# Part of the block attention moved into the projection loop of a hybrid decoder layer

## The chip, the cores and the metric

The kernel runs on all 8 cores of one Trainium2 chip. Each core computes one batch element and no data pass between cores. The metric is the device time of the slowest core, in microseconds (us).

## The reference, cut to what matters

For one batch element, `x` is 2048 tokens by 1024 features. One input projection of 5120 columns feeds three head groups (mLSTM, MoBA block attention, attention to 256 memory tokens). Each group is multiplied by a SiLU gate, the results are concatenated, and one output projection and a layer norm follow. The change touches the MoBA group:

```
proj = x @ w_in
x_m, z_m, q_a, k_a, v_a, z_a, q_c, z_c = split_cols(proj)
qa, ka = rotary(q_a), rotary(k_a)                  # 4 heads of 128
# keys in 8 blocks of 256; each query sees its own block (causal) and the
# 3 past blocks with the largest q . mean(k of the block)
out_a = moba_attention(qa, ka, va) * silu(z_a)
```

A query in the first four blocks has at most three past blocks, so for tokens 0 to 1023 nothing has to be selected. Selection concerns tokens 1024 to 2047 only.

## The kernel before, in words

The kernel is written with a small scheduler (class `Sched`): each call of `S.add` appends an instruction to the list of one engine, in the order in which the Python code runs, and puts in the semaphore waits that reads and writes of named tiles ask for. So each engine runs its instructions in program order, and an instruction that waits holds up everything behind it on its engine. All matmuls go through `mm` (L233), all activations through `act` (L236), and most DMAs through `dma` (L239), so many rows carry the line of a helper.

The work of a core comes in five parts with barriers between them: (1) the projections for MoBA, then the MoBA attention itself (up to L555); (2) memory attention (to L638); (3) the rest of the mLSTM projections; (4) convolution and gates; (5) the mLSTM recurrence and the output. The change is in part 1 alone.

**Projections** (L387 to L400). `fm_tile` makes one tile of 128 features by 512 tokens with 8 matmuls into one of PSUM banks 0 to 3, in turn; `va_tile` makes a V tile of 128 tokens by 512 features in the same way. `j` counts four chunks of 512 tokens, `c` four groups of features (for `fm_tile` one head each). A Q tile (`wA`, `evq`) or K tile (`wC`, `evk`) is evacuated by `ev_rot`: three VectorE products with the cosine and sine tables (L367 to L369, PSUM and SBUF in), then one GpSimd addition (L370, both inputs in SBUF) that writes `qa` or `ka`. A V tile is copied by ScalarE (L385). A gate tile (`wD`, `evz`) is evacuated by ScalarE with SiLU. Chunk 0 is made first, then for `j` = 1 to 3 and `c` = 0 to 3 one tile each of Q, V, K and gate.

**Attention** (L431 to L553). `T` counts four chunks of 512 queries. For each `T` and head there are 2(2T+1) items 'w' (128 keys against the 512 queries) and one item 'n' (the last 256 keys against the upper 256 queries): 3, 7, 11 and 15 items a head, 144 in all, 40 of them with T below 2. An item is: scores (one matmul, plus causal masks, plus for T of 2 and 3 a matmul with `esel` that adds the selection mask `selT`), an exponential on ScalarE into `Ebuf`, a PV matmul into bank 6, and an addition into `Esum` on VectorE (L531 to L540). Scores run two items ahead, in banks 0 to 2. After each head comes the head end (L546 to L553): a matmul with ones sums `Esum` over partitions (bank 7), ScalarE takes Ln, copies bank 6 to `osb` and takes Exp, and VectorE makes the two products L550 and L552.

**Work laid between the items.** `selection` emits the block selection in steps of 4 operations in each of the first 38 items: 4 reductions of `ka` (L403), 32 small matmuls, 32 MAX8 (L414), and at item 38 the rest, 32 transposes and 4 copies of `selT` (L420, L422; some of them earlier). `fill(1)` emits, from item 8, one matmul per item of the 128 that make the memory group's `qc`. `warm(1)` emits, once selection is done, a matmul per item whose result nobody reads.

The softmax here doesn't subtract the row's maximum and nothing guards it: scores larger than these inputs give would overflow.

## Time and profile before

| what | value |
|---|---|
| median of 3 runs | 1054.05 us (1053.66 to 1123.73) |
| the profiled execution | 1053.22 us |
| its span on the slowest core, from the first to the last instruction | 1050.8 us (cores: 1041.5 to 1050.8 us) |
| part 1: projections of chunks 1 to 3 | 55.03 to 138.20 us of the span |
| part 1: items with T below 2 and selection | 138.20 to 229.60 us |
| part 1: items with T of 2 and 3 | 229.60 to 399.20 us |

The profile is one execution on the slowest core. Busy time counts what an engine executes; the time that an instruction waited is given beside it with what ended the wait. Times in a row are microseconds from the start of the span, and durations in ns where the row gives a mean. The bounds inside part 1 are read from the order of the matmuls: the last projection tile, the first score matmul of T = 2, the last PV matmul.

### The profile page before, as it was taken

The page shows a single profiled execution, that of the slowest core. Times are in us where ns is not written, and L with a number is a line of the kernel's source. Part 1 is how long each engine was busy: PE and PEld are TensorE (multiplying, and loading weights), DVE is VectorE, ACT ScalarE, POOL GpSimd, SP SyncE. Part 2 cuts the span into 40 slices and gives each one's busy share as a digit, 9 for nine tenths or more (in the row PEclk, how much of TensorE's full clock was granted, in tenths as well). Part 3 has the DMA queues.
Part 4 walks back from the last instruction along what each step waited for, and adds up shares of the span by engine and source line. Part 5 has one row for each costly group of instructions (what it writes and reads, how often), then busy time and mean ns, then how long its engine had stood idle before and what let it go on. Part 6 is the DMA issues. An engine that isn't in the chain of part 4 may idle for free.

```text
span 1050.8 us, 13469 instructions; the slowest of 8 cores (1041.5 to 1050.8 us)
## 1 busy us (share of the span) xinstructions
PE 825.4 (79%) x3779; PEld 367.1 (35%) x3849; DVE 505.1 (48%) x1060; ACT 411.6 (39%) x807; POOL 187.8 (18%) x151
## 2 busy tenths in 40 slices
PE   1999956579888888998999895756666666489994
PEld 0444422222322223443444353323333333234441
DVE  4555674444555552065100201686666667545452
ACT  2111123344444443375133634555545555512121
POOL 8233320000000001001000000000101121327765
PEclk9999977897999999999999987686765666689997
DMA  9930050000000005700600100000000028035552
GB/s 156 157 49 0 1 80 1 0 1 1 1 0 1 1 1 77 104 1 11 101 1 1 65 1 0 1 1 1 1 1 1 1 34 128 0 111 166 145 160 101
DMA packets 26648, 43.72 MB, mean 42 GB/s; under 512 B 1744, under 2 KB 19280, under 8 KB 26448
## 3 DMA queue, kind: packets, MB, share of 16 engines
q0 software_dynamic: 20368, 23.33, 15.3%
q1 hardware_dynamic: 6208, 19.53, 6.2%
q8 instruction: 33, 0.54, 0.2%
q14 instruction: 39, 0.32, 0.1%
HBM read 56.75 MB, written 8.39 MB: 62 GB/s over the span
## 4 chain that ended last, share of the span: by engine, by line
PE 65%; DVE 11%; ACT 10%; issue 8%; DMA 4%; POOL 1%; DVEq 1%; ACTq 0%; POOLq 0%
PE ps L233 63%; ACT arena L236 8%; DMA arena<-w_in 4%; DVE arena L819 2%; DVE arena L866 1%; PE ps L861 1%; ACT arena L829 1%; DVE arena L811 1%; DVE arena L403 1%; DVE arena L540 1%; DVE arena L785 1%; DVE arena L780 1%; DVE arena L533 1%; ACT arena L822 1%; DVEq L129 1%
## 5 line engine op out<-in xcount | busy, mean ns | idle before, releaser
L233 PE MATMUL ps<-arena 128*128 128x512 bf16 (+6 forms) x3194 | 727.2, 369 | 143.8 <-ACT arena L236 34.7
L233 PEld LDWEIGHTS ps<-arena 128*128 128x128 bf16 (+2 forms) x3248 | 320.8, 106 | 526.6 <-issue 270.4
L236 ACT ACTIVATE arena<-ps 128x512 bf16<-128x512 f32 (+1 forms) x274 | 155.6, 595 | 231.6 <-PE ps L233 217.9
L236 ACT ACTIVATE arena<-arena 128x256 bf16<-128x256 f32 (+6 forms) x138 | 85.3, 654 | 115.1 <-DVE arena L920 87.5
L533 DVE TENSOR_TENSOR arena<-arena 128x512 f32<-128x512 f32 x112 | 77.5, 692 | 45.2 <-ACT arena L236 38.1
L233 PE MATMUL ps<-triAB,ident 128*128 128x512 bf16 (+1 forms) x230 | 91.2, 401 | 1.8 <-issue 0.8
L301 DVE CAST arena<-ps 128x512 bf16<-128x512 f32 (+2 forms) x59 | 35.6, 611 | 105.7 <-PE ps L233 103.2
L822 ACT CAST arena<-arena 128x257 bf16<-128x257 f32 x120 | 47.6, 409 | 67.9 <-DVE arena L819 56.0
L870 POOL TENSOR_TENSOR arena<-arena 128x512 bf16<-128x512 f32 x32 | 36.3, 1154 | 204.6 <-DVE arena L866 204.6
L299 ACT CAST arena<-ps 128x512 bf16<-128x512 f32 (+2 forms) x59 | 30.3, 521 | 74.8 <-PE ps L233 67.8
L370 POOL TENSOR_TENSOR arena<-arena 128x512 bf16<-128x512 f32 x32 | 40.5, 1266 | 73.3 <-DVE arena L369 73.3
L239 POOL DMA_DIRECT2D arena<-w_kv x2 | 1.8, 888 | 264.0 <-issue 264.0
L819 DVE SCALAR_TENSOR_TENSOR arena<-arena,ps 128x257 f32<-128x257 f32 x112 | 48.5, 475 | 0.0
L861 PE MATMUL ps<-ident,arena 128*128 128x128 bf16 x128 | 19.9, 264 | 33.6 <-ACT arena L236 27.5
L927 POOL TENSOR_TENSOR arena<-arena 128x1024 f32<-128x1024 f32 x16 | 37.6, 2348 | 44.9 <-ACT arena L236 44.9
L916 DVE SCALAR_TENSOR_TENSOR arena<-arena,ps 128x512 f32<-128x512 f32 x32 | 22.0, 686 | 44.5 <-PE ps L233 44.5
L367 DVE TENSOR_TENSOR arena<-ps,arena 128x512 f32<-128x512 f32 x32 | 22.1, 692 | 41.7 <-PE ps L233 41.6
L866 DVE SCALAR_TENSOR_TENSOR arena<-ps,normg_s,arena 128x512 f32<-128x512 bf16 x32 | 24.0, 751 | 37.5 <-PE ps L233 27.6
L928 POOL TENSOR_TENSOR arena<-arena 128x1024 f32<-128x1024 f32 x16 | 37.6, 2350 | 2.4 <-POOL arena L927 0.2
L550 DVE TENSOR_TENSOR arena<-arena 128x512 f32<-128x512 f32 x16 | 11.1, 692 | 55.5 <-ACT arena L236 55.5
L233 PE MATMUL ps<-arena,esel 8*128 8x512 bf16 (+1 forms) x96 | 36.5, 380 | 0.3
L233 PE MATMUL ps<-arena,ones 128*128 128x512 f32 (+1 forms) x34 | 22.8, 762 | 17.5 <-DVE arena L540 17.3
(108 smaller groups left out, 516.3 us busy)
## 6 DMA issues: line engine op xcount, KB each, us to landing
arena<-w_in POOLq DMA_DIRECT2D x10, 1024.0 KB, 18.6
arena<-x SPq DMA_DIRECT2D x16, 512.0 KB, 5.5
y<-arena SPq DMA_DIRECT2D x16, 512.0 KB, 4.0
arena<-xT POOLq DMA_DIRECT2D x4, 1024.0 KB, 45.2
arena<-w_out POOLq DMA_DIRECT2D x4, 1024.0 KB, 18.4
arena<-w_kv POOLq DMA_DIRECT2D x2, 1024.0 KB, 16.4
arena<-pos POOLq DMA_DIRECT2D x1, 1024.0 KB, 6.9
arena<-memT POOLq DMA_DIRECT2D x1, 512.0 KB, 13.1
```

The costliest lines, as they stand in the source:

```text
L233: S.add('pe', lambda e: e.matmul(out, lhsT, rhs, start=start, stop=stop), reads, writes)
L236: S.add(eng, lambda e: e.activation(out=out, in_=in_, func=func, **kw), reads, writes)
L301: S.add('dve', lambda e: e.tensor_copy(dst_ap, src_ap), reads, writes)
L370: S.add('pool', lambda e: e.tensor_tensor(dst[:, c, sl], rt1[:, k, :], rt2[:, k, :], ALU.add), [('rt1', k), ('rt2', k, 0), ('rt2', k, 1)], ...
L533: S.add('dve', lambda e, ke=ke, fi=fi: e.tensor_tensor(Esum[:, fi, :], Esum[:, fi, :], Ebuf[:, ke, :], ALU.add), [('E', ke), ('Esum', fi)] ...
L819: S.add('dve', lambda e, dc=dc, bD=bD: e.scalar_tensor_tensor(C32[:, dc, 0:257], C32[:, dc, 0:257], gdec[:, col:col + 1], ps[bD][:, 0:257] ...
L822: S.add('act', lambda e, dc=dc: e.copy(Cbf[:, i % 2, dc, 0:257], C32[:, dc, 0:257]), [('C32', dc)], [('Cbf', i % 2, dc)])
L861: S.add('pe', lambda e, ci=ci, ec=ec, sl_=sl_: e.transpose(pTb[:, sl_], hnb[:, kb, ci, ec * P:(ec + 1) * P], ident[:]), [('hnb', kb, ci), ...
L866: S.add('dve', lambda e, ec=ec, c=c, pv=pv: e.scalar_tensor_tensor(tg[:, ec, :].rearrange("p (ci t) -> p ci t", ci=4), pv, normg[:, c:c + ...
L870: S.add('pool', lambda e, ec=ec, c=c: e.tensor_tensor(cat[:, c, gsl], tg[:, ec, :], cat[:, c, gsl], ALU.mult), [('tg', ec), ('cat', c, g4) ...
L927: S.add('pool', lambda e, k=k: e.tensor_tensor(yb[:, k, :], yb[:, k, :], lngb, ALU.mult), [('yb', k), 'lngb'], [('yb', k)])
L928: S.add('pool', lambda e, k=k: e.tensor_tensor(yb[:, k, :], yb[:, k, :], lnbb, ALU.add), [('yb', k), 'lnbb'], [('yb', k)])
```

## The change

The items, unchanged in what they compute, become objects (`MobaRun`) that can be stepped from elsewhere. The order of part 1 becomes: chunk 0 as before; the 4 gate tiles of chunk 1; then, for `j` = 1 to 3, one tile of Q, V and K per `c`, 36 tiles, each wrapped around one item with T below 2 (exponential and `Esum` additions ahead of the tile, next scores and PV behind it); the 4 items that are left; the 8 gate tiles of chunks 2 and 3; then the last head end, the selection with 48 of the 128 `qc` matmuls in its middle, and at last the 104 items with T of 2 and 3, each with one `qc` matmul while there are any, and one `warm` matmul. Items with T below 2 use banks 4 and 5 and run one item ahead; their head end is emitted behind the next item. `Ebuf` is used in four slots instead of three, and the copy to `osb` is emitted ahead of Ln instead of behind it. The first six `qc` tiles are copied by ScalarE. The number of matmuls that make results is unchanged; `warm` goes from 106 to 104.

```
-        for j in range(1, 4):
-            for c in range(4):
-                fm_tile(wA, 'wA', evq, c, j)
-                va_tile(j * 4 + c)
-                fm_tile(wC, 'wC', evk, c, j)
-                fm_tile(wD, 'wD', evz, c, j)
+        gate_tiles_left = []
+        runA = MobaRun(moba_items([0]), [4, 5], 1)
+        runB = MobaRun(moba_items([1]), [4, 5], 1)
+        for c in range(4):
+            fm_tile(wD, 'wD', evz, c, 1)
+        for j in range(1, 4):
+            for c in range(4):
+                for tile_fn in (lambda: fm_tile(wA, 'wA', evq, c, j), lambda: va_tile(j * 4 + c),
+                                lambda: fm_tile(wC, 'wC', evk, c, j)):
+                    run = runB if runA.done() else runA
+                    run.pre()
+                    tile_fn()
+                    run.post()
+        for j in range(2, 4):
+            for c in range(4):
+                if not runB.done():
+                    runB.step()
+                gate_tiles_left.append((c, j))
+        for c, j in gate_tiles_left:
+            fm_tile(wD, 'wD', evz, c, j)
...
-        LA = 2
-        fin = 0
-        for q_ in range(LA):
-            scores(q_)
-        for idx, (kind, h, T, n, half) in enumerate(items):
-            selection(4 if idx + LA < 40 else 10 ** 6)
-            if idx + LA < len(items):
-                scores(idx + LA)
-            if idx >= 8:
-                fill(1)
-            if sel_state[0] >= len(sel_ops):
-                warm(1)
...
+        while pending:
+            pending.pop(0)()
+        items = moba_items([2, 3])
+        selection(67)
+        fill(48)
+        selection(10 ** 6)
+        runC = MobaRun(items, [0, 1, 2], 2)
+
+        def hookC(idx):
+            fill(1)
+            warm(1)
+
+        while not runC.done():
+            runC.step(hookC)
```

The new methods, and the head end as it is emitted now (`pending` is flushed behind the next item's PV matmul):

```
+            def pre(self):
...
+                self.ke = mstate['slot'] % 4
+                mstate['slot'] += 1
+                moba_exp(self.its[self.pos], self._bank(self.pos), self.ke)
+                if adds_early:
+                    moba_adds(self.its[self.pos], self.ke, mstate['fin'] % 2)
...
+            def post(self):
...
+                idx = self.pos
+                if idx + self.LA < len(self.its):
+                    scores(self.its[idx + self.LA], self._bank(idx + self.LA))
+                moba_all(self.its[idx], self._bank(idx), self.ke, True)
+                self.pos += 1
...
+                S.add('act', lambda e: e.copy(osb[:, fi, :], ps[6][:]), [('ps', 6)], [('osb', fi)])
+
+                def head_end():
+                    mm(ps[7][:], ones32[:], Esum[:, fi, :], True, True, ['ones32', ('Esum', fi)], [('ps', 7)])
+                    act(rden2[:, fi, :], ps[7][:], AF.Ln, [('ps', 7)], [('rden2', fi)])
+                    act(rden2[:, fi, :], rden2[:, fi, :], AF.Exp, [('rden2', fi)], [('rden2', fi)], scale=-1.0)
...
+                if T < 2:
+                    pending.append(head_end)
+                else:
+                    head_end()
```

On VectorE, the place where the Q and K tiles of the last two chunks are evacuated. Before, the three products of one tile follow those of the next (the rows go on so up to the reductions of the selection):

```order
L367 TENSOR_TENSOR arena<-ps,arena 128x512
L368 TENSOR_TENSOR arena<-ps,arena 64x512
L369 TENSOR_TENSOR arena<-ps,arena 64x512
L367 TENSOR_TENSOR arena<-ps,arena 128x512
L368 TENSOR_TENSOR arena<-ps,arena 64x512
L369 TENSOR_TENSOR arena<-ps,arena 64x512
```

The same engine and place in the changed kernel, in the first head of T = 1. L434 and L439 are the additions into `Esum` (L533 and L540 before):

```order
L434 TENSOR_TENSOR arena<-arena 128x512 x2
L367 TENSOR_TENSOR arena<-ps,arena 128x512
L368 TENSOR_TENSOR arena<-ps,arena 64x512
L369 TENSOR_TENSOR arena<-ps,arena 64x512
L434 TENSOR_TENSOR arena<-arena 128x512
L367 TENSOR_TENSOR arena<-ps,arena 128x512
L368 TENSOR_TENSOR arena<-ps,arena 64x512
L369 TENSOR_TENSOR arena<-ps,arena 64x512
L434 TENSOR_TENSOR arena<-arena 128x512 x2
```

The additions now stand between the tiles: two ahead of every K tile, one ahead of every Q tile.

On TensorE, the end of the projections. Before, the attention began right behind the last tile, with small selection matmuls (128x8) among the first items:

```order
L233 MATMUL ps<-arena 128x512 x513
L233 MATMUL ps<-triAB,ident 128x256
L233 MATMUL ps<-arena 128x512
L233 MATMUL ps<-triAB,ident 128x256
L233 MATMUL ps<-arena 128x256
L233 MATMUL ps<-triAB,ident 128x256
L233 MATMUL ps<-arena 128x256
L233 MATMUL ps<-triAB,ident 128x256
L233 MATMUL ps<-arena 128x512 x2
L233 MATMUL ps<-triAB,ident 128x256
L233 MATMUL ps<-arena 128x512
L233 MATMUL ps<-arena 128x8 x4
```

Behind the last leftover item the changed kernel has the 8 gate tiles, the last head end's ones matmul, the selection's matmuls, 6 `qc` tiles, the transposes (L593 here), and the first scores of T = 2:

```order
L233 MATMUL ps<-arena 128x512 x64
L233 MATMUL ps<-arena,ones 128x512
L233 MATMUL ps<-arena 128x8 x32
L233 MATMUL ps<-arena 128x512 x48
L593 MATMUL ps<-ident,arena 8x128 x32
L233 MATMUL ps<-arena 128x512
L233 MATMUL ps<-arena,esel 128x512
```

The selection moved out of the items into one piece, with only the 48 `qc` matmuls inside it.

## Rows read from the trace of the kernel before

**Rows 1.** Busy time by stretch: length, then PE, PEld, DVE, ACT, POOL, PEclk, DMA, GB/s.
```profile
55.03:138.20 83.17, 82.75 (x380) 37.72 (x387) 49.84 (x74) 14.28 (x25) 30.39 (x24) 1.00 0.08 11
138.20:229.60 91.40, 53.76 (x239) 22.33 (x242) 50.48 (x105) 37.79 (x67) 3.04 (x3) 0.81 0.16 24
229.60:399.20 169.60, 148.76 (x565) 48.12 (x574) 86.36 (x137) 75.11 (x136) 0.00 (x0) 0.95 0.00 1
399.20:405.40 6.20, 1.28 (x5) 0.34 (x4) 2.05 (x4) 1.60 (x3) 0.00 (x0) 1.00 0.00 0
```

**Rows 2.** Groups by form, 138 to 395 us: count, busy us, mean ns, idle before.
```profile
L533 DVE TENSOR_TENSOR arena<-arena 128x512 f32<-128x512 f32 x108 | 74.7, 692 | 44.3 <-ACT arena L236 37.4 <-issue 0.3
...
L540 DVE TENSOR_TENSOR arena<-arena 128x256 f32<-128x256 f32 x30 | 12.8, 425 | 7.5 <-ACT arena L236 4.9
...
L550 DVE TENSOR_TENSOR arena<-arena 128x512 f32<-128x512 f32 x15 | 10.4, 692 | 52.5 <-ACT arena L236 52.5
...
L403 DVE TENSOR_REDUCE arena<-arena 128x8 f32<-128x2048 bf16 x4 | 9.1, 2282 | 0.0
...
L531 DVE CAST arena<-arena 128x512 f32<-128x512 bf16 x16 | 6.7, 422 | 0.0
...
L414 DVE MAX8 arena<-arena 128x8 f32<-128x8 f32 x32 | 5.4, 168 | 2.5
...
L422 ACT COPY arena<-ps 8x1024 bf16<-8x1024 bf16 x4 | 4.0, 1002 | 4.4 <-PE ps L420 4.4
```

**Rows 3.** Timeline of DVE, one rotated tile and the next tile's first product.
```profile
28.75 0.69 DVE L367 TENSOR_TENSOR arena<-ps,arena 128x512 f32<-128x512 f32 x1
29.54 0.69 DVE L368 TENSOR_TENSOR arena<-ps,arena 64x512 f32<-64x512 f32 x1
30.34 0.68 DVE L369 TENSOR_TENSOR arena<-ps,arena 64x512 f32<-64x512 f32 x1
31.06 0.69 DVE L367 TENSOR_TENSOR arena<-ps,arena 128x512 f32<-128x512 f32 x1
```

**Rows 4.** Line L370, GpSimd's addition: duration ns min/median/max.
```profile
L370 POOL TENSOR_TENSOR arena<-arena x32: 1261/1267/1272, 28.9 to 138.9; 128x512 bf16<-128x512 f32 x32
```

**Rows 5.** Timeline, 12.5 to 17.5 us: VectorE and GpSimd side by side.
```profile
12.88 2.29 DVE L312 TENSOR_TENSOR arena<-arena 128x2048 f32<-128x2048 f32 x1
...
13.21 2.12 POOL L252 TENSOR_SCALAR_AFFINE_SELECT ident<-ident 128x128 f32<-128x128 f32 x1
...
15.96 1.10 POOL L259 TENSOR_SCALAR_AFFINE_SELECT U<-U 128x128 f32<-128x128 f32 x1
```

**Rows 6.** Timeline of ACT, the table load between the last SiLU and the first exponential.
```profile
138.74 1.28 ACT L236 ACT_TABLE_LOAD   x1
140.03 1.58 ACT L236 ACTIVATE arena<-ps 128x512 bf16<-128x512 f32 x3
```

**Rows 7.** Timeline of PE at the end of a head of T = 2.
```profile
273.67 1.02 PE L233 MATMUL ps<-arena,ones 128*128 128x512 f32 x2
...
277.02 0.59 PE L233 MATMUL ps<-arena 128*128 128x512 bf16 x2 [1.26 <-ACT arena L236]
```

**Rows 8.** Timeline of ACT at the same head end: Ln, copy, Exp, next exponentials.
```profile
274.79 0.60 ACT L236 ACTIVATE arena<-ps 128x512 f32<-128x512 f32 x1 [3.38 <-PE ps L233]
275.28 0.58 ACT L548 COPY arena<-ps 128x512 f32<-128x512 f32 x1
275.75 0.64 ACT L236 ACTIVATE arena<-arena 128x512 f32<-128x512 f32 x1
```

**Rows 9.** Busy time of three short stretches, columns as in rows 1.
```profile
142.00:150.00 8.00, 0.38 (x4) 0.09 (x1) 7.58 (x9) 0.00 (x0) 0.00 (x0) 0.75 1.13 168
...
234.00:248.00 14.00, 13.22 (x27) 2.93 (x28) 5.46 (x10) 5.45 (x10) 0.00 (x0) 0.53 0.00 0
258.00:266.00 8.00, 5.48 (x22) 1.64 (x22) 3.84 (x7) 4.25 (x9) 0.00 (x0) 1.00 0.00 0
```

**Rows 10.** Timeline of PE, the last ones matmul with T below 2.
```profile
234.38 1.67 PE L233 MATMUL ps<-arena,ones 128*128 128x512 f32 x2 [0.75 <-DVE arena L540]
```

More of the change, by code:

```diff
@@ new lines, in build_nc, with moba_exp, moba_adds @@
+        mstate = {'fin': 0, 'slot': 0}
+        pending = []
+        def moba_exp(item, b, ke):
+            act(Ebuf[:, ke, :], ps[b][:], AF.Exp, [('ps', b)], [('E', ke)], scale=SC128)
+        def moba_adds(item, ke, fi):
+            kind, h, T, n, half = item
+            if kind == 'w':
+                if n == 0 and half == 0:
+                    S.add('dve', lambda e: e.tensor_copy(Esum[:, fi, :], Ebuf[:, ke, :]), [('E', ke)], [('Esum', fi)])
+                else:
+                    S.add('dve', lambda e: e.tensor_tensor(Esum[:, fi, :], Esum[:, fi, :], Ebuf[:, ke, :], ALU.add),
+                          [('E', ke), ('Esum', fi)], [('Esum', fi)])
+            else:
+                for hf in range(2):
+                    hs = slice(hf * 256, (hf + 1) * 256)
+                    S.add('dve', lambda e, hs=hs: e.tensor_tensor(Esum[:, fi, 256:512], Esum[:, fi, 256:512], Ebuf[:, ke, hs], ALU.add),
+                          [('E', ke), ('Esum', fi)], [('Esum', fi)])
@@ new lines, in moba_all, with __init__, _bank, done @@
+        def moba_all(item, b, ke, early=False):
+            due = list(pending)
+            del pending[:]
+            moba_body(item, b, ke, early)
+            for f in due:
+                f()
+        class MobaRun:
+            def __init__(self, its, banks, LA):
+                self.its, self.banks, self.LA, self.pos, self.started = its, banks, LA, 0, False
+            def _bank(self, idx):
+                return self.banks[idx % len(self.banks)]
+            def done(self):
+                return self.pos >= len(self.its)
+            def pre(self):
+                if self.done():
+                    return
+                if not self.started:
+                    for q_ in range(min(self.LA, len(self.its))):
+                        scores(self.its[q_], self._bank(q_))
+                    self.started = True
+                self.ke = mstate['slot'] % 4
+                mstate['slot'] += 1
+                moba_exp(self.its[self.pos], self._bank(self.pos), self.ke)
+                if adds_early:
+                    moba_adds(self.its[self.pos], self.ke, mstate['fin'] % 2)
+            def post(self):
+                if self.done():
+                    return
+                idx = self.pos
[3 more added lines that the diff above has]
+                self.pos += 1
+            def step(self, hook=None):
+                if self.done():
+                    return
+                if not self.started:
+                    for q_ in range(min(self.LA, len(self.its))):
+                        scores(self.its[q_], self._bank(q_))
+                    self.started = True
+                idx = self.pos
+                if idx + self.LA < len(self.its):
+                    scores(self.its[idx + self.LA], self._bank(idx + self.LA))
+                if hook is not None:
+                    hook(idx)
+                ke = mstate['slot'] % 4
+                mstate['slot'] += 1
+                moba_all(self.its[idx], self._bank(idx), ke)
+                self.pos += 1
@@ L429, in selection @@
                     sel_state[0] += 1
-        items = []
-        for T in range(4):
-            for h in range(4):
-                for n in range(2 * T + 1):
-                    items.append(('w', h, T, n, 0))
-                    items.append(('w', h, T, n, 1))
-                items.append(('n', h, T, 2 * T + 1, 0))
         NB = 3
@@ L469, in fill @@
                     if kind == 'qc':
-                        copy_evac(qc[:, c, sl], ps[b][:], [('ps', b)], [('qc', c, j), 'wC', 'wD'])
+                        if fstate['u'] < 6:
+                            S.add('act', lambda e, dst=qc[:, c, sl], src=ps[b][:]: e.copy(dst, src), [('ps', b)], [('qc', c, j), 'wC', 'wD'])
+                        else:
+                            copy_evac(qc[:, c, sl], ps[b][:], [('ps', b)], [('qc', c, j), 'wC', 'wD'])
                     else:
@@ L554, in build_nc @@
+        while pending:
[10 more added lines that the diff above has]
+            runC.step(hookC)
+        while pending:
+            pending.pop(0)()
         fill(10 ** 6)
```

124 lines of the change are left out of this document (67 added, 57 removed).

## The prediction

> **What bounds the kernel now.** I read the stretches first, then the groups by form, then the timeline at the seams. In the projection stretch TensorE is busy 82.75 of 83.17 us at clock 1.00, so it is the bound there; VectorE is busy 49.84 us, ScalarE 14.28 and GpSimd 30.39 [rows 1]. In the next 91.40 us, which hold the 40 items with T below 2 and the selection, TensorE works only 53.76 us, part of it at a low clock (mean 0.81), and no other engine is busy for more than 50.48 us [rows 1]: a chain of waits is the bound there. From 229.60 us on TensorE is the bound again, 148.76 of 169.60 us [rows 1]. The idea of the change can be read off this: the items go into the stretch where ScalarE and VectorE have room. What has to be asked is whether that room is enough, and what the selection costs when it stands alone.
>
> **The slot loop: TensorE's side.** The old stretch is 48 tiles in 83.17 us, 1.73 us each [rows 1], or 0.217 us per matmul of 512 columns. The 36 tiles of the new loop are 62.4 us. An item 'w' at T = 1 is 2 such matmuls (2.5 with a mask), an item 'n' 3, so a head is 16, or 3.5 us, and 1.0 us for the ones matmul [rows 7]; a head of T = 0 is 8, 1.7 us, and 1.0. The slots hold four heads of T = 0 (10.9 us) and 24 of the 28 items of T = 1 (3.4 heads, 15.4 us). Sum: 89 us.
>
> **VectorE's side.** A rotated tile takes 31.06 - 28.75 = 2.31 us [rows 3]; 24 of them are 55.4 us. An addition takes 0.69 us, the two halves of item 'n' 0.85, the first item's copy 0.42, each head-end product 0.69 [rows 2]; between dependent instructions there is another 0.1 us [rows 3]. So a head of T = 1 is 0.5 + 5 x 0.78 + 1.0 + 1.5 = 6.9 us and one of T = 0 3.8 us: 15.2 and 23.5 us. Sum: 94 us. VectorE becomes the bound of this loop, a little above TensorE. ScalarE, with 36 exponentials of 0.53 us (1.58 for three [rows 6]) and little else, is far below.
>
> **A wait that the old loop did not have.** In the first microseconds GpSimd's select on a 128x128 float tile took 2.12 us while VectorE ran a product with both inputs in SBUF from 12.88 to 15.17 us, and a like one 1.10 us a little later [rows 5]; it ended 0.16 us after VectorE did. The two do not run side by side. The old tile products take one input from PSUM, and GpSimd's additions beside them keep to 1261 to 1272 ns [rows 4]. The additions into `Esum` have both inputs in SBUF and now stand right behind the tiles, where GpSimd's addition starts. Ahead of a K tile there are two: the first gets ahead of GpSimd, the second finds GpSimd's 1.27 us in front of it. Behind a K tile there is one, and GpSimd's addition then lies beside the next tile's products, which costs nothing. From below the price is 0, from above all 24 additions, 24 x 1.27 = 30.5 us; I take one of 1.0 us in each of 12 rounds, 12 us. The loop is then 106 us on VectorE. TensorE can be some 4 us ahead of it at the end, as four banks allow two tiles in hand, so I count 102 us.
>
> The Trainium skill, "SBUF — State Buffer", section "SBUF: two separate sides", calls the pair of ports that VectorE and GpSimd share an exclusive lock, taken by whichever instruction starts first, for the whole of it, where VectorE has two SBUF inputs. The rows above agree for a VectorE instruction that came first; none shows GpSimd's coming first against such an addition. By that rule every GpSimd addition could hold VectorE up, which is the third case below.
>
> **Around the loop.** Gate tiles of chunk 1 come first: 4 x 1.73 = 6.9 us. The 4 leftover items run one behind the other (scores, exponential, PV): about 1 us each, 4 us, between 2 and 8. Then 8 gate tiles, 13.9 us. Nothing of VectorE's reductions hides under these tiles, though `ka` is complete: the last head end is emitted ahead of the selection, its two products wait for Ln and Exp, these for the ones matmul, and that stands behind the 64 gate matmuls.
>
> **The selection alone.** From the last gate matmul: the last SiLU 0.6 (as Ln, [rows 8]), a table load 1.28 [rows 6], Ln and Exp about 1.1 [rows 8], two products 1.5, four reductions of 2.28 with their scalings, 9.8 [rows 2], then the last 8 small matmuls, in all 15.5 us in which TensorE has next to nothing. Then 48 `qc` matmuls: 10.4 us at full clock, and more at its start, since the clock falls in a long wait: over the 8 us from 142 it was 0.75 with 0.38 us of work [rows 9]. I take 13. The 32 MAX8, 5.4 us of work [rows 2], lie beside them. Then the transposes and copies of four heads on one bank, 1.0 us a copy [rows 2] and as much again for transposes and hand-over: 8 us, the last copy beside the first scores, 7 on the path. Sum: 35.5 us, between 31 and 43.
>
> The Trainium skill, "ScalarE: Activation LUTs", section "What ACT_TABLE_LOAD costs", puts a drain of about 1.38 us on top of the load. Here the next exponential began 0.01 us after the load ended [rows 6], so the measurement decides for no drain; by the page the sum would be an estimated 1.4 us longer.
>
> **Items with T of 2 and 3.** These took 169.60 us [rows 1]. Some 5 us of that belong to the last two items of T = 1 and their head end (the ones matmul alone ended at 236.05 [rows 10]). Of the `qc` matmuls 80 instead of 96 are left: 16 x 0.217 = 3.5 us. At each of 8 head ends the copy to `osb` stood between Ln and Exp, 0.47 us [rows 8], on the path of the next exponential for which TensorE waited 1.26 us [rows 7]; now it runs while the ones matmul is awaited: 3.8 us. About 1 us goes with a `qc` copy that ScalarE has no longer to make here. So 156.3 us. I leave the clock as it was: 0.53 for 14 us early in the stretch [rows 9], some 7 us that may go, come back, or double.
>
> **Edits at nothing.** The fourth slot of `Ebuf` frees a wait that no row shows. The reload of `wA` and `wB` still waits for GpSimd's last addition and the last Q tile; its 2 MB move at some 168 GB/s [rows 9], 12.5 us, and the first `qc` matmul now comes behind the leftover items, the gate tiles and the reductions, over 30 us later. Without that cover the `qc` matmuls, and the transposes behind them, would wait for it.
>
> **Sum.** 55.0 + 6.9 + 102 + 4 + 13.9 + 35.5 + 156.3 = 373.6 us for the end of the last PV matmul, against 399.2: 25.6 us earlier. All behind it is unchanged and starts at the same barrier. The profiled execution took 1053.22 us, 0.8 below the median of 1054.05. 1053.2 - 25.6 = 1027.6, and I say 1027, 2.6% below the median. About 2% (21 us, 1033) is what a measurement of this kernel can tell from no change. So the forecast's own margin is only 6 us, and its own spread, from the leftover items, the selection and the clock, is 10 us to either side.
>
> **The rivals.**
> *The ports cost nothing.* If GpSimd always gives way, the loop is 94 us on VectorE and 90 on TensorE, 12 less: 1015 us. For it: rows 4 show an addition that was never slowed in the old loop. Against it: nothing there had two SBUF inputs at that time.
> *The loop is full.* If each of the 24 GpSimd additions stops VectorE for its 1.27 us, 30.5 instead of 12 us, the end moves by 18.5: 1046 us, the same within 2%. The items are then hidden from TensorE's view but most of the gain is spent on VectorE. For it: the two engines meet 24 times. Against it: at half of these VectorE has only one such instruction.
> *The clock falls in the slots (slower).* TensorE works 89 of 102 us there, with a wait in most slots. If these waits bring the clock to half all through the loop, as in the stretch from 234 us (0.53 [rows 9]), the 89 us become 178, TensorE is the bound, and the kernel takes 1027 + 76 = 1103 us. It becomes slower than before once 26 us are lost; the 13 us that TensorE idles take up the first 13, so its work must stretch by 39 us, a clock at half for nearly half of the loop. For it: mean 0.81 from 138 to 229 us [rows 1]. Against it: from 258 to 266 us TensorE was busy 5.48 of 8 us and kept 1.00 [rows 9], and here the waits are short.
>
> **Chances.** Forecast 0.46, ports free 0.26, loop full 0.21, clock 0.07. Of the forecast's case 0.7 lies below 1033: 0.32, with the ports-free case 0.58, and a little from the third, 0.60. Same: 0.14 from the first, 0.19 from the third, 0.33. Slower 0.07. The range 1009 to 1048 takes in the first three with the bounds of the selection on the outer ones cut, and leaves out the clock's case.
>
> **What would show it.** Right: in the changed profile the stretch from 62 us on has VectorE busy nine tenths and more, GpSimd's addition longer than 1.27 us in the loop or VectorE's addition longer than 0.69, TensorE at clock 1.00 and idle some 13%; then a hole of about 15 us behind the gate tiles, ended by the reductions; T = 2 begins near 217 us. Wrong: additions of 0.69 us throughout (ports free), a granted clock well below 1.00 in the loop, selection longer than 43 us, or T of 2 and 3 longer than before.

## The result and the profile after

The changed kernel takes 1025.41 us (median of 12 runs, 1023.32 to 1029.25) against 1054.05 us for the kernel before; the ratio is 0.9727, 95% interval 0.9709 to 0.9744. It is faster by 2.7%; the forecast was 1027 us. The profiled execution took 1026.14 us. Here and in the table of the experiments a median is over all executions of a kernel, while a ratio leaves out those in which the cores of one die ran at a lower clock throughout or that lay more than 1.5% above the fastest.

Part 1 by stretches, on the core of the profile. The columns are those of [rows 1]: bounds, length, then PE, PEld, DVE, ACT, POOL, granted clock, DMA share, GB/s. The stretches are the slot loop, the four leftover items, the eight gate tiles, the selection, the items with T of 2 and 3.

```profile
66.20:166.30 100.10, 91.62 (x419) 42.02 (x417) 87.37 (x124) 40.34 (x72) 36.66 (x23) 0.97 0.00 1
166.30:169.45 3.15, 2.23 (x13) 0.95 (x12) 2.93 (x5) 2.24 (x4) 0.00 (x0) 1.00 0.00 0
169.45:183.28 13.83, 13.83 (x66) 6.37 (x65) 4.49 (x6) 5.94 (x9) 3.48 (x3) 1.00 0.64 84
183.28:217.41 34.13, 17.02 (x115) 8.44 (x114) 17.45 (x45) 9.63 (x13) 0.00 (x0) 0.77 0.17 28
217.41:372.10 154.69, 141.28 (x551) 45.84 (x550) 82.66 (x130) 74.96 (x131) 0.00 (x0) 0.96 0.00 1
```

Part 1 now ends its last PV matmul at 372.10 us, 27.1 us earlier than before (399.20 [rows 1]), and the execution is 27.1 us shorter (1053.22 to 1026.14): behind part 1 little came or went (651.6 us of the span before, 652.5 now, on the two profiled cores). In the loop VectorE is busy 87 of 100 us and TensorE 92, where before no stretch had both of them near full [rows 1].

VectorE in the loop, grouped by form (count, busy us, mean ns, idle before). Of before, [rows 2] has the same operations under other lines: additions 692 and 425 ns, the first product 692 ns; the second product, which has no row there, took 692 ns too:

```profile
L552 DVE TENSOR_TENSOR arena<-arena 128x512 bf16<-128x512 f32 x15 | 10.4, 692 | 1.6
```

After:

```profile
L434 DVE TENSOR_TENSOR arena<-arena 128x512 f32<-128x512 f32 x19 | 15.0, 787 | 1.5 <-ACT arena L236 0.9
L439 DVE TENSOR_TENSOR arena<-arena 128x256 f32<-128x256 f32 x14 | 9.4, 672 | 1.4 <-DVE arena L434 0.2
L482 DVE TENSOR_TENSOR arena<-arena 128x512 bf16<-128x512 f32 x7 | 9.2, 1320 | 0.7
L480 DVE TENSOR_TENSOR arena<-arena 128x512 f32<-128x512 f32 x7 | 5.8, 827 | 1.5 <-ACT arena L236 1.2
```

All four, and only these, have both inputs in SBUF, and all four have grown. Together they take 39.4 us; at their lengths of [rows 2] they would take 19 x 0.692 + 14 x 0.425 + 14 x 0.692 = 28.8. So 10.6 us went into waits inside the instructions. One such place on VectorE's timeline, with a pair without a stall 7 us earlier:

```profile
108.01 1.48 DVE L434 TENSOR_TENSOR arena<-arena 128x512 f32<-128x512 f32 x2
...
111.70 0.69 DVE L434 TENSOR_TENSOR arena<-arena 128x512 f32<-128x512 f32 x1
112.31 0.68 DVE L367 TENSOR_TENSOR arena<-ps,arena 128x512 f32<-128x512 f32 x1
...
114.61 2.37 DVE L434 TENSOR_TENSOR arena<-arena 128x512 f32<-128x512 f32 x2
116.91 0.68 DVE L367 TENSOR_TENSOR arena<-ps,arena 128x512 f32<-128x512 f32 x1
```

The other side of it on GpSimd's timeline:

```profile
114.72 1.71 POOL L370 TENSOR_TENSOR arena<-arena 128x512 bf16<-128x512 f32 x1 [1.20 <-DVE arena L369]
```

and its line over the whole kernel (duration ns min/median/max), to set beside [rows 4]:

```profile
L370 POOL TENSOR_TENSOR arena<-arena x32: 1261/1447/1716, 29.6 to 170.4; 128x512 bf16<-128x512 f32 x32
```

Read together: VectorE's first addition starts at 114.61, GpSimd's at 114.72 and it takes 0.44 us more than the 1.27 of [rows 4]; VectorE's pair takes 2.37 instead of 1.48 us, 0.89 more, while GpSimd runs till 116.43. Each engine has been held up once by the other.

VectorE begins the loop with the first row below. The next two rows show its only waits over 0.2 us in the loop, and the last row is the last product of the 36th tile:

```profile
68.92 0.43 DVE L432 CAST arena<-arena 128x512 f32<-128x512 bf16 x1 [9.58 <-ACT arena L236]
...
144.90 0.77 DVE L480 TENSOR_TENSOR arena<-arena 128x512 f32<-128x512 f32 x1 [1.19 <-ACT arena L236]
...
150.87 0.79 DVE L434 TENSOR_TENSOR arena<-arena 128x512 f32<-128x512 f32 x1 [0.88 <-ACT arena L236]
...
169.54 0.68 DVE L369 TENSOR_TENSOR arena<-ps,arena 64x512 f32<-64x512 f32 x1
```

From 68.92 to 170.22 us are 101.3 us; 2.1 of them are these waits and 10.6 the time lost inside instructions. VectorE's own work, with the short gaps between instructions, is the other 88.6 us.

TensorE pays for this at the ones matmul, which needs `Esum` complete. Its timeline at two of the heads of T = 1, and then the busy time of the 4.7 us from the second on (columns of [rows 1]):

```profile
121.17 1.10 PE L233 MATMUL ps<-arena,ones 128*128 128x512 f32 x2 [3.26 <-DVE arena L439]
...
141.34 2.04 PE L233 MATMUL ps<-arena,ones 128*128 128x512 f32 x2 [3.26 <-DVE arena L439]
```

```profile
141.30:146.00 4.70, 4.66 (x9) 1.71 (x10) 3.20 (x6) 1.71 (x3) 1.27 (x1) 0.50 0.00 0
```

Before, the ones matmul of [rows 7] waited for nothing and that of [rows 10] for 0.75 us. Over the loop such waits for additions add up to 7.8 us, at four of the seven ones matmuls. After the second wait the ones matmul itself takes 2.04 instead of 1.10 us: the granted clock is 0.50 there, the lower of the two levels (1.2 of 2.4 GHz).

The selection alone, on TensorE, ScalarE and VectorE:

```profile
183.28 1.02 PE L233 MATMUL ps<-arena,ones 128*128 128x512 f32 x2
191.31 0.41 PE L233 MATMUL ps<-arena 128*128 128x8 bf16 x8 [7.01 <-DVE arena L578]
193.68 0.38 PE L233 MATMUL ps<-arena 128*128 128x8 bf16 x8 [1.96 <-DVE arena L578]
196.14 0.37 PE L233 MATMUL ps<-arena 128*128 128x8 bf16 x8 [2.09 <-DVE arena L578]
198.63 12.15 PE L233 MATMUL ps<-arena 128*128 128x8 bf16 x56 [2.12 <-DVE arena L578]
210.71 0.61 PE L593 MATMUL ps<-ident,arena 128*8 128x128 bf16 x8
212.67 0.61 PE L593 MATMUL ps<-ident,arena 128*8 128x128 bf16 x8 [1.35 <-ACT arena L595]
```

```profile
184.38 1.28 ACT L236 ACT_TABLE_LOAD   x1 [0.24 <-PE ps L233]
185.68 0.60 ACT L236 ACTIVATE arena<-ps 128x512 f32<-128x512 f32 x1
186.37 0.63 ACT L236 ACTIVATE arena<-arena 128x512 f32<-128x512 f32 x1
```

```profile
187.10 0.69 DVE L480 TENSOR_TENSOR arena<-arena 128x512 f32<-128x512 f32 x1 [12.62 <-ACT arena L236]
187.89 0.69 DVE L482 TENSOR_TENSOR arena<-arena 128x512 bf16<-128x512 f32 x1
188.50 2.28 DVE L576 TENSOR_REDUCE arena<-arena 128x8 f32<-128x2048 bf16 x1
```

VectorE idles 12.62 us, although the reductions' inputs were complete, because two products stand ahead of them in its queue. TensorE's 7.01, 1.96, 2.09 and 2.12 us of waiting are the hole that was forecast.

### The profile page after: what moved, and what is told of

Read it like the earlier page. It is cut to its first block, busy times and chain, and to the rows that moved or that the text cites. A ratio compares the mean times of both kernels' runs of the same rounds, so it can differ in the third digit from the quotient of the medians.

```text
span 1024.6 us, 13518 instructions; the slowest of 8 cores (1017.8 to 1024.6 us)
## 1 busy us (share of the span) xinstructions
PE 821.2 (80%) x3836; PEld 366.2 (36%) x3836; DVE 511.6 (50%) x1057; ACT 420.5 (41%) x812; POOL 195.8 (19%) x151
## 4 chain that ended last, share of the span: by engine, by line
PE 68%; DVE 10%; ACT 9%; issue 7%; DMA 4%; POOL 1%; DVEq 0%; ACTq 0%; POOLq 0%
PE ps L233 66%; ACT arena L236 6%; DMA arena<-w_in 4%; DVE arena L934 2%; DVE arena L981 1%; PE ps L976 1%; ACT arena L944 1%; DVE arena L926 1%; DVE arena L576 1%; DVE arena L900 1%; DVE arena L895 1%; DVE arena L439 1%; ACT arena L937 1%; DVE arena L947 1%; DVEq L129 0%
## 5 line engine op out<-in xcount | busy, mean ns | idle before, releaser
L434 DVE TENSOR_TENSOR arena<-arena 128x512 f32<-128x512 f32 x112 | 80.2, 716 | 37.9 <-ACT arena L236 31.3
L301 DVE CAST arena<-ps 128x512 bf16<-128x512 f32 (+2 forms) x56 | 33.4, 607 | 103.0 <-PE ps L233 102.1
L985 POOL TENSOR_TENSOR arena<-arena 128x512 bf16<-128x512 f32 x32 | 36.3, 1154 | 204.0 <-DVE arena L981 204.0
L370 POOL TENSOR_TENSOR arena<-arena 128x512 bf16<-128x512 f32 x32 | 48.5, 1515 | 96.4 <-DVE arena L369 96.4
L824 DVE TENSOR_SCALAR arena<-ident,convw_s 128x128 bf16<-128x128 bf16 x32 | 7.5, 254 | 59.9 <-ACT arena L236 57.3
L480 DVE TENSOR_TENSOR arena<-arena 128x512 f32<-128x512 f32 x16 | 12.0, 751 | 37.5 <-ACT arena L236 37.2
```

Of the source, the lines that this page charges most:

```text
L301: S.add('dve', lambda e: e.tensor_copy(dst_ap, src_ap), reads, writes)
L370: S.add('pool', lambda e: e.tensor_tensor(dst[:, c, sl], rt1[:, k, :], rt2[:, k, :], ALU.add), [('rt1', k), ('rt2', k, 0), ('rt2', k, 1)], ...
L434: S.add('dve', lambda e: e.tensor_tensor(Esum[:, fi, :], Esum[:, fi, :], Ebuf[:, ke, :], ALU.add), [('E', ke), ('Esum', fi)], [('Esum', fi)])
L985: S.add('pool', lambda e, ec=ec, c=c: e.tensor_tensor(cat[:, c, gsl], tg[:, ec, :], cat[:, c, gsl], ALU.mult), [('tg', ec), ('cat', c, g4) ...
```

## The experiments

Each ratio is to runs of the kernel before on the same chip at the same time. Since the time is that of the slowest of eight cores, I also read the stretches on every core, from TensorE's timeline: `S1` from the first mask matmul of the slots to the ones matmul ahead of the selection (loop, leftover items, eight gate tiles), `S2` from there to the first matmul with `esel` (selection), `S3` from there to the last mask matmul (items with T of 2 and 3). Medians over the cores, the longest `S3`, and the span's median:

| kernel | time, us | ratio (95%) | S1 | S2 | S3 (longest) | span |
|---|---|---|---|---|---|---|
| changed kernel | 1025.41 | 0.9727 (0.9709 to 0.9744) | 116.8 | 35.1 | 153.7 (153.8) | 1019.2 |
| e1_no_adds | 1016.15 | 0.9645 (0.9626 to 0.9663) | 105.7 | 35.8 | 153.1 (155.4) | 1011.7 |
| e2_one_input | 1027.62 | 0.9747 (0.9723 to 0.9772) | 112.1 | 36.0 | 154.0 (160.4) | 1019.2 |
| e9_one_input_all | 1015.68 | 0.9636 (0.9619 to 0.9652) | 106.1 | 35.9 | 152.4 (155.4) | 1012.2 |
| e5_spread | 1029.35 | 0.9732 (0.9703 to 0.9761) | 115.3 | 35.9 | 152.6 (153.6) | 1019.5 |
| e3_sel_first | 1020.04 | 0.9681 (0.9661 to 0.9700) | 116.6 | 23.8 | 152.5 (157.9) | 1010.9 |
| e4_copy_behind | 1029.99 | 0.9762 (0.9744 to 0.9780) | 116.7 | 35.6 | 155.0 (157.9) | 1026.5 |
| e8_no_slots | 1048.20 | 0.9949 (0.9929 to 0.9969) | | | | 1044.8 |
| e6_both | 1011.96 | 0.9566 (0.9539 to 0.9593) | 125.9 | 12.1 | 143.4 (154.9) | 999.8 |
| e12_both_again | 1020.38 | 0.9672 (0.9636 to 0.9707) | 125.9 | 12.1 | 142.6 (167.0) | 998.5 |
| e10_sel_order | 1021.94 | 0.9690 (0.9676 to 0.9705) | 127.4 | 12.1 | 146.8 (166.4) | 1004.0 |
| e11_order_again | 1019.80 | 0.9692 (0.9669 to 0.9714) | 127.4 | 12.1 | 157.4 (166.5) | 1012.5 |

In the last four kernels a part of the selection stands ahead of that ones matmul, so only S1 + S2 compares. In them 24 more of the `qc` matmuls, 5.2 us at 0.217 us each [rows 1], stand ahead of S3.

The intervals don't hold all of the spread: one and the same kernel came to 0.9566 on one chip (e6) and to 0.9672 on another (e12). So a difference of 1% between two rows is told by the stretches, not by the times.

**e1_no_adds: no additions in the slots.** Of the sums only the first item's copy stays.

```
-                if adds_early:
+                if self.its[self.pos][3] == 0 and self.its[self.pos][4] == 0 and self.its[self.pos][0] == 'w':
                     moba_adds(self.its[self.pos], self.ke, mstate['fin'] % 2)
```

> The changed kernel without the 32 additions into Esum that stand in the 36 slots of the projection loop (the first copy of each head stays); the sums that normalise tokens below 1024 are left out by this, nothing else. Theory (VectorE, with its waits for GpSimd, sets the loop's length): VectorE loses 32 additions or pairs of them and most stalls, TensorE's own 90 to 92 us become the bound, the loop goes from 100.1 to about 91 us and the time from 1025 to about 1016 us. Rival (TensorE and its waits for exponentials already set the loop): the loop stays at 100 us and the time at 1025 us within 2 us.

The slots lose the additions of 28 items, not 32. S1 fell by 11.1 us, the time by 9.3. VectorE's additions, with what holds them up, set the length of the loop. This doesn't yet tell work from waits.

**e2_one_input: additions of the same length with one input.** The sums of T below 2 are left out by this too.

```
-                    moba_adds(self.its[self.pos], self.ke, mstate['fin'] % 2)
...
+                    S.add('dve', lambda e, ke_=ke_: e.tensor_reduce(km32[:, 0, 0:1], Ebuf[:, ke_, :], AX.X, ALU.add), [('E', ke_)], [('km32', 0)])
...
```

> The changed kernel with each of those additions replaced by a reduction of the same tile that reads one SBUF input instead of two and should take about the same 0.69 us on VectorE; the sums that normalise tokens below 1024 are left out by this. Theory (the ports shared with GpSimd cost 0.88 us at 13 places, 8 of them at an addition): the stalls at the additions go, 8 x 0.88 = 7 us, those at the head-end products stay; loop about 93 to 95 us, time about 1019 us. GpSimd's addition returns to 1.27 us at most places. Rival (it is VectorE's work and not the ports): loop 100 us, time 1025 us.

S1 fell by 4.7 us only. The additions' stand-ins ran undisturbed, but the head-end products kept their collisions, which grew from 5.3 to 6.3 us; VectorE in the loop, by form:

```profile
L521 DVE TENSOR_REDUCE arena<-arena 128x1 f32<-128x512 bf16 x21 | 14.3, 682 | 0.8
L482 DVE TENSOR_TENSOR arena<-arena 128x512 bf16<-128x512 f32 x7 | 10.1, 1446 | 0.7
L480 DVE TENSOR_TENSOR arena<-arena 128x512 f32<-128x512 f32 x7 | 5.9, 845 | 0.3
```

The time didn't follow at all: in the profiled execution two cores, the slowest one among them, needed 160.4 us for the items with T of 2 and 3, the others 152.7 to 155.9 (below). The run left open how much of e1's gain was work, so the products had to go too.

**e9_one_input_all: the products with one input as well.**

```
+                    if T < 2:
+                        S.add('dve', lambda e: e.tensor_reduce(t2c[:, fi, 0:1], rden2[:, fi, :], AX.X, ALU.add),
+                              [('rden2', fi), ck], [('t2c', fi)])
+                        S.add('dve', lambda e: e.tensor_reduce(km32[:, 0, 1:2], osb[:, fi, :], AX.X, ALU.add),
+                              [('osb', fi), ('t2c', fi)], [ck, ('km32', 0)])
+                        return
...
```

> As e2, and the two products at each head end with T below 2 are replaced as well by one-input reductions of 512 columns (0.69 us each); so no VectorE instruction of the loop has two inputs in SBUF, while their number and length stay. Left out: the sums Esum of T below 2 and the division by them. Theory (the port lock sets the loop, e2 left a third of it standing at the products): the stretch from the first mask matmul to the ones matmul ahead of the selection, 116.8 us in the changed kernel and 112.1 in e2, comes to 105 to 107, the floor that e1 found, with every VectorE instruction at its own length and GpSimd's additions at 1.27 us; time 1014 to 1019 us. Rival (VectorE's mere work sets the loop, 94 us of it, the lock only adds at the seams): the stretch stays at 110 to 112 us, time 1020 to 1026.

S1 fell to 106.1 us, 10.7 less than in the changed kernel, and the time to 1015.68 us, with as many VectorE instructions of the same length in the loop. VectorE's groups by form in the loop:

```profile
L527 DVE TENSOR_REDUCE arena<-arena 128x1 f32<-128x512 bf16 x21 | 14.4, 686 | 1.5
...
L481 DVE TENSOR_REDUCE arena<-arena 128x1 f32<-128x512 f32 x7 | 4.8, 686 | 0.2
L483 DVE TENSOR_REDUCE arena<-arena 128x1 f32<-128x512 f32 x7 | 4.8, 686 | 0.7
L432 DVE CAST arena<-arena 128x512 f32<-128x512 bf16 x8 | 3.8, 474 | 9.1 <-ACT arena L236 8.9
```

and GpSimd's addition, min/median/max:

```profile
L370 POOL TENSOR_TENSOR arena<-arena x32: 1260/1268/1701, 30.4 to 161.3; 128x512 bf16<-128x512 f32 x32
```

and one of these additions that started beside a copy (L432):

```profile
77.60 1.44 POOL L370 TENSOR_TENSOR arena<-arena 128x512 bf16<-128x512 f32 x1 [3.10 <-DVE arena L369]
```

None of the reductions is stretched, GpSimd's median is back at 1268 ns, no wait of TensorE in the loop is over 0.4 us, and the loop stands at TensorE's own work: 106.1 less the 3.15 and 13.83 us of the two stretches behind it are 89.1 us. One input alone is not what frees an instruction: the copy that begins a head, which has one too, took 474 ns in the mean instead of 422 [rows 2], and GpSimd's addition took 1.44 us beside it in 6 places, in the changed kernel as well.

e1, e2 and e9 have one thing more in common: `Esum` is not summed, so the ones matmuls wait for no addition. Between e2 and e9 this is alike and only the products differ: their collisions, 6.3 us, go, and S1 falls by 6.0. From the changed kernel to e2 the collisions fall from 10.6 to 6.3 us, by 4.3, and S1 by 4.7. So the collision of the two engines, not VectorE's work (88.6 us, beside TensorE's 89.1), is nearly all of the 10.7 us that the loop pays on top. A loop without collisions whose ones matmuls still wait for the additions was run in another order only, that of e5.

**e5_spread: the additions and products put off.** In rounds with a K tile they are emitted behind the next tile's first products, where GpSimd's addition should be over; `drain` emits them ahead of the third product of the next rotated tile. The two products of a head end are put off in the same way.

```
+                drain()
                 S.add('dve', lambda e: e.tensor_tensor(rt2[64:128, k, :], pst[0:64, :], sinS[64:128, sl], ALU.mult), [pkey, 'sinS1'], [('rt2', k, 1)])
...
+                if put_off:
+                    later.append(lambda: moba_adds(*args))
+                else:
+                    moba_adds(*args)
```

> The changed kernel with the same VectorE instructions in another order: in the loop the additions of a K tile's item, and both products of a head end, are emitted between the second and third product of the next rotated tile, so that only one instruction with two SBUF inputs follows a tile. Theory (ports): GpSimd's addition lies beside the tile's products, the 13 stalls of 0.88 us go, loop about 91 to 93 us, time about 1017 us. Rival (VectorE's work, not the order, or TensorE, sets the loop): 100 us and 1025 us.

Mostly a miss. The stalls are nearly gone (products 693 and 678 ns, additions 743 and 532 with those of the leftover items), but S1 fell by 1.5 us only. TensorE now meets a wait at nearly every ones matmul, since the sums that it needs come later:

```profile
85.59 1.10 PE L233 MATMUL ps<-arena,ones 128*128 128x512 f32 x2 [1.26 <-DVE arena L446]
...
122.21 1.10 PE L233 MATMUL ps<-arena,ones 128*128 128x512 f32 x2 [1.07 <-DVE arena L446]
...
140.68 1.10 PE L233 MATMUL ps<-arena,ones 128*128 128x512 f32 x2 [1.55 <-DVE arena L446]
```

and VectorE in turn waits 9.3 us for tiles. Taking the collision away is worth 10.7 us where no matmul waits for the additions (e9), and 1.5 where it is bought with a later `Esum`.

**e3_sel_first: eight selection steps, the four reductions with their scalings, ahead of the last head end.**

```
+        selection(8)
         while pending:
             pending.pop(0)()
...
-        selection(67)
+        selection(59)
```

> The changed kernel with the selection's 4 reductions and 4 scalings emitted ahead of the last head end instead of behind it. Theory (the hole of 15 us behind the gate tiles is VectorE's reductions, queued behind two products that wait for matmul, Ln and Exp): the reductions run beside the gate tiles, the hole shrinks to 1 or 2 us, and the transposes wait for the 32 MAX8 instead of the qc matmuls; 10 to 13 us less, about 1014 us. Rival (the selection's chain on VectorE is as long either way, only its place moves): at most 4 us less, 1021 us or more.

S2 fell by 11.3 us, as expected: in TensorE's timeline the 7.01 us wait is gone and one of 3.11 us ahead of the transposes is left. The time fell by 5.4 us only, as three cores took some 158 us for the items with T of 2 and 3.

**e4_copy_behind: the copy to `osb` behind Ln again, for T of 2 and 3.**

```
-                S.add('act', lambda e: e.copy(osb[:, fi, :], ps[6][:]), [('ps', 6)], [('osb', fi)])
+                if T < 2:
+                    S.add('act', lambda e: e.copy(osb[:, fi, :], ps[6][:]), [('ps', 6)], [('osb', fi)])
...
                     act(rden2[:, fi, :], ps[7][:], AF.Ln, [('ps', 7)], [('rden2', fi)])
+                    if T >= 2:
+                        S.add('act', lambda e: e.copy(osb[:, fi, :], ps[6][:]), [('ps', 6)], [('osb', fi)])
```

> The changed kernel with the copy to osb put back behind Ln for the 8 heads with T of 2 and 3. Theory (the copy stood on the path from the ones matmul to the next exponential): 8 x 0.47 = 3.8 us slower, about 1029 us, and TensorE waits 1.26 us again behind the head end. Rival (the copy lies beside waiting anyway): no change, 1025 us within 1 us.

S3 rose by 1.3 us in the median core and by 4 in the longest; TensorE's waits for ScalarE's exponentials in it are 15.1 us against 12.6 in the changed kernel (on the profiled cores, over 155 us each). The sign is as the prediction has it, the 3.8 us are not reached. The time rose by 4.6 us, of which the medians have 2.7 in the unchanged rest (652.7 against 650.0): that it met the expected 1029 us is in good part not the copy's doing.

**e8_no_slots: the same order without the interleaving.** The 40 items run one after the other between the tiles and the gate tiles.

```
-                    run = runB if runA.done() else runA
-                    run.pre()
                     tile_fn()
-                    run.post()
...
+        for run in (runA, runB):
+            while not run.done():
+                run.step()
```

> The changed kernel with the 40 items of T below 2 taken out of the slots and run one behind the other after the 36 tiles, all else kept (gate tiles moved, selection in one piece, 48 qc matmuls in it). Theory (the gain is the items' latency hidden beside the tiles): the 36 tiles take 62 us, the items about 1.1 us each and 1.5 us a head end, 56 us; 118 us instead of 103.2, so 15 us or more slower than the changed kernel, 1040 to 1050 us, most of the gain gone. Rival (the gain comes from the selection in one piece and the later items): within 5 us of 1025 us.

1048.20 us: of 28.6 us gained, 22.8 go when the items don't lie in the tiles, and the other edits are left with some 6.

**e6_both and e10_sel_order: the selection taken apart.** The selection is emitted ahead of the last head end, with 40 `qc` matmuls in its waits and 8 more behind each head's transposes; e6 has e5's edit as well, e10 has not.

```
+        items = moba_items([2, 3])
+        selection(75)
+        fill(40)
         while pending:
             pending.pop(0)()
-        items = moba_items([2, 3])
-        selection(67)
-        fill(48)
-        selection(10 ** 6)
+        for _ in range(4):
+            selection(9)
+            fill(8)
```

> The order of e5, and the selection taken apart: reductions, small matmuls and the whole VectorE chain emitted ahead of the last head end, 40 qc matmuls behind the small matmuls, and 8 more between the transposes of one head and the next (72 of the 128 instead of 48 ahead of T of 2). Theory: 8 us from the loop, 12 to 13 from the hole behind the gate tiles, 4 to 5 from TensorE's waits between the transposes, since those qc matmuls are work that no longer stands between the items; about 1001 us. Rival (the gains overlap, as the transposes wait for the 32 MAX8 and the two products): 1008 to 1012 us.

> The selection order of e6 alone (selection operations and 40 qc matmuls ahead of the last head end, the rest of qc between the transposes), without e5's put-off additions and products. Theory (e6's gain is the order, e5's part is worth its 1.4 us of the stretch and no more): stretch plus selection 139.5 us against 138.0 in e6 and 151.9 in the changed kernel, the items with T of 2 and 3 in 143 us where the clock holds, time 1011 to 1017 us. Rival (the put-off additions carried a part of it): stretch plus selection 142 or more, time 1018 to 1022.

S1 + S2 is 151.9 us in the changed kernel, 138.0 in e6 and 139.5 in e10: e5's edit is worth 1.5 us in it, as by itself. In S3 TensorE now starts at full clock, and a core that keeps it takes 142.3 to 142.6 us instead of 153.7. Of these 11 us, 5.2 are the 24 `qc` matmuls that no longer stand there; the other 6 fit the stretch with which the changed kernel begins S3, at a low clock: 35 matmuls in 14 us (columns as above), where core 5 of e10 has 54 in its first 14 us at 1.00:

```profile
217.41:231.41 14.00, 14.00 (x35) 3.39 (x35) 4.58 (x7) 5.42 (x9) 0.00 (x0) 0.59 0.00 0
```

e6 missed its expectation of about 1001 us and came out at its rival's 1008 to 1012. e10's time missed its expectation (1011 to 1017 us) too, and e6's ten us of lead over it, measured on another chip, are not in S1 + S2. Two cores of e10 in the same execution show where the time went, core 4 and then core 5, in the same 16 us (columns as above; busy alike, but 33 matmuls at clock 0.58 against 60 at 1.00):

```profile
301.00:317.00 16.00, 14.79 (x33) 3.07 (x34) 8.11 (x13) 6.60 (x12) 0.00 (x0) 0.58 0.01 2
...
301.00:317.00 16.00, 14.81 (x60) 4.81 (x59) 9.71 (x16) 9.21 (x16) 0.00 (x0) 1.00 0.01 2
```

**e11_order_again, e12_both_again: chance or kernel?** The kernels of e10 and e6 once more, both on one chip.

> The kernel of e10 once more, beside e6's in one job. In e10 the items with T of 2 and 3 took 142.3 us on three cores, all at clock 1.00, and 166.4 on core 4. Theory (the order of the work decides little, which core loses its clock in this stretch and for how long is chance): other cores than 4 and 6 are the long ones this time, and the time of single runs varies by 5 us and more. Rival (it belongs to the kernel, or to the core): core 4 is again the longest by over 8 us, and the time is again 1020 to 1023 us.

> The kernel of e6 once more, beside e10's in one job. Theory (e6 and e10 differ by 1.5 us of work, the rest of their distance of 10 us is clock): the two medians lie within 4 us of each other once both have had their runs, or where they do not, the distance of the slowest cores stands in the stretch with T of 2 and 3 at a lower granted clock. Rival (the put-off additions are worth 10 us by themselves): the distance of some 10 us comes again and stands in the stretch up to the selection.

In e10 the long S3 were those of cores 4 (166.4) and 6 (157.3); in e11 core 4 had 142.3, and cores 1, 3 and 7 had 163.5 to 166.5. In e6 the longest was core 4's (154.9), in e12 core 5's (167.0), where core 4 had 142.6. So neither the core nor the put-off additions decide it. This time the medians, 1019.80 and 1020.38, lie 0.6 us apart, so e6's lead over e10 at first is not established as a lead of the kernel. Against the expectation, e10's time came out within 3 us both times: in each of the four profiled executions of this order at least one core had a long S3 (the longest 154.9 to 167.0 us), and it sets the time. Core 5 of e12, where S3 was 167.0 us, in three pieces of it:

```profile
205.00:225.00 20.00, 17.92 (x75) 6.04 (x73) 9.60 (x16) 9.61 (x18) 0.00 (x0) 1.00 0.00 0
...
305.00:325.00 20.00, 20.00 (x53) 5.28 (x52) 6.90 (x11) 6.06 (x11) 0.00 (x0) 0.59 0.00 1
325.00:345.00 20.00, 18.81 (x52) 4.43 (x52) 9.94 (x15) 8.86 (x16) 0.00 (x0) 0.66 0.00 0
```

The order takes 12.4 to 13.9 us out of S1 + S2 in the median core, with 5.2 us of `qc` work more in it. The time of the slowest core shows less of that: the four ratios are 0.957 to 0.969 against 0.973, where e11's interval overlaps that of the changed kernel and e10's ends just below it (0.9705 against 0.9709). How far below 1020 us it can be had depends on a clock that these runs don't control.

## Why the prediction was right

Step by step, in us, on the profiled core:

| step | predicted | measured |
|---|---|---|
| chunk 0 and four gate tiles, start of the loop | 61.9 | 66.2 |
| slot loop | 102 | 100.1 |
| leftover items | 4 | 3.15 |
| eight gate tiles | 13.9 | 13.83 |
| selection | 35.5 | 34.1 |
| items with T of 2 and 3 | 156.3 | 154.7 |
| end of the last PV matmul | 373.6 | 372.1 |

- **The loop.** Its mechanism held: VectorE is the bound, with GpSimd's additions in front of its two-input instructions. 12 x 1.0 us were taken for that, and 10.6 us in the rows and 10.7 in e9 are paid. TensorE's 89 us is what e1 and e9 fall back to, and its lead at the end, put at 4 us, is 3.9 (166.30 against 170.22). But that 102 came so near to 100.1 is in part luck. VectorE's own work was put at 94 us and is 88.6: the prediction gave every addition 0.78 us, while behind an addition the next tile's product starts after 0.61 (111.70 to 112.31 in the timeline above). Against these 5.4 us too much stand 4.8 that were not in the sum: VectorE begins 2.7 us after TensorE's loop (68.92 against 66.20), and waits 2.1 us. And the products at the head end carry half of the stalls, 5.3 of 10.6 us (L482 and L480), where the prediction gave all 12 to the additions.
- **The signs.** GpSimd's and VectorE's longer additions, the hole of 15 us ended by the reductions and the start of T = 2 (217.41 us, forecast near 217) came as named. Three came in part: VectorE busy 87% instead of nine tenths and more, TensorE idle 8% instead of 13, and a mean clock of 0.97 instead of 1.00.
- **The rule on the ports.** The Trainium skill, "SBUF — State Buffer", section "SBUF: two separate sides", has the pair of ports held by whichever instruction starts first. That GpSimd's coming first holds VectorE up, which no row of before showed, is now seen (0.89 us), as is the reverse (1.71 instead of 1.27 us). That every GpSimd addition would stop VectorE, the rival of the full loop, isn't: 10.6 us are about 12 stalls of 0.89 in 23 additions of GpSimd.
- **The rivals.** "The ports cost nothing" gave 1015 us; the kernel without the collision takes 1015.68 us (e9). So the rival's price was right and its condition wrong. The clock fell only once for long in the loop, behind the 3.26 us wait that ended at 141 us (0.50 over the next 4.7 us).
- **The selection.** 15.3 us from the last ones matmul to the last wait's end at 198.63 (predicted 15.5; the pieces named for it add up to 14.3 and eight small matmuls, and the ones matmul of 1.02 us ahead of Ln is not among them), then `qc` and transposes in 18.8 (20). That the head end holds the reductions up is shown by e3: 11.3 us go when they stand ahead of it. The table load was followed by Ln after 0.02 us, so the drain of 1.38 us that the Trainium skill, "ScalarE: Activation LUTs", section "What ACT_TABLE_LOAD costs", adds is not seen here either.
- **T of 2 and 3.** The sum came out, but not all by its terms: the copy ahead of Ln is worth 1.3 us in the median core by e4, not 3.8, and the clock, left as it was, was 0.96 instead of 0.95 [rows 1]; the 14 us at 0.53 early in it [rows 9] came back as 14 us at 0.59. The stretch came out 1.6 us below its forecast although the copy gave 2.5 less; what makes up these 4 us was not taken apart.
- **The start.** On this core chunk 0 ended 4.3 us later than on the core profiled before, in code that hasn't changed; the cores start the loop between 61.5 and 66.3 us. Before, the first mask matmul came at 137.9 to 142.4 us on the eight cores, and the profiled one, at 138.1, was among the early ones. That takes back most of what the other steps came out below their forecasts.

## What to carry to other kernels

When work is moved beside an engine that shares something with it, count the instructions that share (here two inputs in SBUF on VectorE beside GpSimd), not only the busy time; then ask whether they can be given one input, before putting them off, since what is put off is waited for elsewhere. (No run here has such a kernel with the same result: e2 and e9 leave out the sums.) What is emitted ahead of a lone stage holds it up even when its inputs are ready: put the stage's first steps ahead of anything that waits. And where eight cores run, look at the granted clock of every core before a small step is counted as gained or lost.

## What the runs showed of the hardware

- A two-input VectorE instruction behind a GpSimd addition stands for 0.89 us longer, and GpSimd's addition behind a two-input VectorE one of 128x512 takes 1.71 instead of 1.27 us. With reductions of one input neither happens (686 and 1268 ns in e9). A one-input copy (bf16 to f32, 0.43 us) does meet GpSimd: 1.44 us for GpSimd's addition beside it.
- With the same program and the same order, cores of one execution differ by up to 24 us in S3 (142.3 and 166.4 in e10), the short ones at clock 1.00 throughout, the long ones at 0.58 to 0.76 for tens of us. In the 16 us ahead of the fall at 301 us TensorE of core 4 of e10 was busy 14.51 us at clock 1.00, that of core 5, which did not fall, 13.58; but in the next 16 us core 5 was busy 14.81 and did not fall either. Which core loses its clock changes from execution to execution; what decides it is open.
